# Final sums of a tile taken bank by bank, and two more places for gathered rows

## The chip, the cores and the metric

One core of one Trainium2 chip. The metric is the device time of one execution in microseconds, as the median of three runs. All numbers of the profile come from one profiled execution of the same program.

## What is computed

One step of an encoder layer for a prompt of 1024 tokens and a sample of 32. After a mixer (an RG-LRU and an mLSTM group, not touched here) comes a mixture of experts with product keys (PEER), then a final RMSNorm:

```python
x = x + g1 * (concat([ya, yb]) @ w_out)
h2 = rmsnorm(x, norm2_w) * (1 + sc2) + sh2
# peer(h2): for each token and each of 8 heads, 16 experts out of 16384
ue = take(u, expert, axis=0)                     # rows of 1024 floats
act = gelu(einsum('phkd,pd->phk', ue, xb))
ve = take(v, expert, axis=0)
out = einsum('phk,phkd->pd', g * act, ve)
y = rmsnorm(x + g2 * out, final_norm_w)
```

Here `g` is the softmax over the 16 chosen scores of a head. Each token reads 8 x 16 = 128 rows of `u` and 128 of `v`; the kernel keeps `u` and `v` of an expert side by side in one table, `peer_uv`, so that one gathered row has 2048 floats, 8 KB.

## The kernel before, in words

The tokens are nine tiles: eight of 128 prompt tokens and one of 32 sample tokens (`NT` = 9). The mixer runs first, for all tiles. After it comes one loop over **slots**, 128 for a prompt tile and 32 for the sample, 1056 in all, written out by each engine for itself in the same order. A slot is one gather by an indirect DMA into one **place** of SBUF: 128 rows, 32 tokens (a quad, `q` = 0 to 3) by four experts of one head, 1 MB. What a slot needs, in order:

- POOL (line 681) waits until the place is free and issues the gather. It waits on `v_free`, which PE counts up per slot, and, at a head's first slot, on `idx_ready`, the expert numbers.
- DVE (`dot`, line 1971) waits for the gather (`e_ld`) and forms the dot products of the 128 `u` rows with the tokens' rows, which stand in `xrep`, spread over the partitions.
- ACT (`weight`, lines 1371 to 1379) makes gelu times gate of it and writes the weights into a small diagonal (`diag`), then ups `dg_ready`.
- PE (`mix`, line 1030) multiplies the `v` halves of the rows by the diagonal with four matmuls and adds them up in PSUM. Quads 0 and 1 add up in bank 0, quads 2 and 3 in bank 1 (`q // 2`). Its last matmul ups `v_free`.

Each queue is in order: a wait of an engine holds everything behind it on that engine. Between the slots each engine has other work of the next tiles, placed by slot number: on DVE the steps that choose the experts (routing, lines 1883 to 1963, one head in 16 slots), on PE the query matmuls (`query`, line 966; scores, index turns) and the replicas (`replicate`, line 1017), which spread the rows of 32 tokens over 128 partitions by two matmuls of 512 columns; ACT copies each into `xrep` (line 1396) before PE makes the next.

The order of slots in a tile is set by `SETS`: for most tiles heads 0 to 3 with quads 0, 1, 2, 3, then heads 4 to 7 with quads 0, 1, 2, 3, each quad of a set being 16 slots. So bank 0 takes slots 0 to 31 and 64 to 95 of a tile, bank 1 slots 32 to 63 and 96 to 127. Tile 1 begins with sets of two heads, there bank 1 is first written in slot 16. `spans[t, i]` lists the slots of tile `t` that go to bank `i`.

There are `RING` = 6 places from the start and two more from slot `JOIN` = 118 on, when the weights that lay in `r_w` are used up; each slot takes the place that was used longest ago.

When a tile's slots are done, its sums go through `final_sum` (after the dot of slot 3 of the next tile; lines 1984 and 1990 are its multiply out of PSUM by `g2` and its add of the `x1` rows), `final_square` (after slot 4, line 1996, with the sum of squares per row), a sum over partitions by PE (`sum_squares`, line 1040, after slot 6), `final_variance` (slot 11), a root by ACT (slot 12), `final_scale` (slot 14, line 2010) and then, on SP (`finish`), eight stores of the tile in 1 KB pieces (line 577) and the loads of the next tile's `x1` rows into `x1s` (line 571). For tile 0 those loads stand on SP's queue behind four loads of query weights for tile 1, 1 MB each, and twelve small ones. The results are written over the tile's normed rows (`h2h(t, 0)` in `r_yT`, `h2h(t, 1)` in `r_vo`), which the replicas read.

What couples the tiles is in `final_sum` and `mix`:

```python
dve.wait_ge(v_free, RING + (t * TILE_SLOTS + TILE_SLOTS if nq == 4 else N_SLOTS))   # final_sum
last.then_inc(acc_free, 1)                       # behind the multiplies of both banks
if t and s == t * TILE_SLOTS:                    # mix, the tile's first slot
    pe.wait_ge(acc_free, t)
```

The line numbers are those of the kernel before; in the changed one they are a few higher (the dot is line 1976, the multiply 1990, the add 1994, the squares 2000, mix 1035, the gather 686).

## Time and profile before

| | us |
|---|---|
| median of three runs (3294.46 to 3301.82) | 3297.12 |
| the profiled execution's own time | 3296.16 |
| its span in the profile | 3294.3 |

The page of the profile gives, for each engine, the busy time as a share of the span; slices, 40 equal parts of the span with the busy share in tenths and the DMA rate; and groups of instructions by source line. Waits are listed by who waited for whom, with total, count and the longest one. A timeline lists single instructions with their start, length and, in brackets, how long the engine had been idle before and what ended that. A window gives the busy time of each engine in a stretch, TensorE's granted clock, the DMA engines' share and their rate. In all of them the places appear under the name of the SBUF tensor they lie in (`r_vo`, `r_yT`, `r_qk`, `r_w`).

### The profile page before, as it was taken

How to read it: one execution, taken by the hardware profiler on the slowest of the kernel's cores; microseconds unless marked ns; L12 is line 12 of the kernel's file. 1: busy time of each engine (PE TensorE's matmuls, PEld its weight loads, DVE VectorE, ACT ScalarE, POOL GpSimd, SP SyncE). 2: the span in 40 equal slices, each digit the busy share in tenths (PEclk: the TensorE clock that was granted, in tenths of full speed). 3: DMA queues.
4: the chain of work that ended last, by engine and by line, in shares of the span. 5: the costliest groups of instructions: out<-in, count | busy, mean ns of one | idle time of the engine just before them, and what ended most of it. 6: DMA issues, size and time to landing. Idle time of an engine off the chain costs nothing.

```text
span 3294.3 us, 46115 instructions
## 1 busy us (share of the span) xinstructions
PE 2306.9 (70%) x15134; PEld 1144.3 (35%) x15134; DVE 2219.6 (67%) x5518; ACT 2000.6 (61%) x6402; POOL 1215.7 (37%) x1118
## 2 busy tenths in 40 slices
PE   7999987988668666666666666666666666666544
PEld 5665464333234333333333233223333332232110
DVE  5687256877667767666766676667666766676645
ACT  3332055777666666666666666666666666666655
POOL 0000102344434444444444444444434444443433
PEclk9999997899656556555655565556556655565555
DMA  7232327999999999999999999999999999999998
GB/s 285 87 104 76 81 72 289 390 392 395 405 385 420 420 420 405 420 420 420 395 420 421 419 399 420 420 420 394 420 420 420 395 420 420 420 397 419 421 421 344
DMA packets 184164, 1195.13 MB, mean 363 GB/s; under 512 B 22122, under 2 KB 32906, under 8 KB 44530
## 3 DMA queue, kind: packets, MB, share of 16 engines
q0 software_dynamic: 154240, 1113.16, 82.5%
q1 hardware_dynamic: 29684, 79.02, 6.8%
q8 instruction: 120, 1.97, 0.3%
q14 instruction: 120, 0.98, 0.1%
HBM read 1182.83 MB, written 9.25 MB: 362 GB/s over the span
## 4 chain that ended last, share of the span: by engine, by line
DMA 49%; PE 24%; ACT 10%; DVE 8%; issue 5%; POOL 3%; SPq 1%; DVEq 0%; POOLq 0%; ACTq 0%
DMA r_w<-in_peer_uv,gidx 21%; DMA r_qk<-in_peer_uv,gidx 12%; DMA r_yT<-in_peer_uv,gidx 11%; PE ps L777 6%; PE ps L1030 5%; PE ps L834 3%; PE ps L966 3%; DMA r_vo<-in_peer_uv,gidx 3%; PE ps L926 2%; PE ps L1017 2%; DVE r_w L1971 2%; ACT mixc L1375 2%; POOL r_vo L681 2%; ACT mixc L1374 1%; DVE r_qk L1971 1%
## 5 line engine op out<-in xcount | busy, mean ns | idle before, releaser
L1371 ACT ACTIVATE mixc<-mixc 128x1 f32<-128x1 f32 x1056 | 212.4, 201 | 797.6 <-DVE r_qk L1971 212.0
L681 POOL DMA_INDIRECT r_vo<-in_peer_uv,gidx x273 | 337.9, 1238 | 647.4 <-PE ps L1030 591.1
L1030 PE MATMUL ps<-r_qk 128*32 128x256 f32 x2192 | 273.1, 587 | 374.9 <-ACT r_qk L1379 334.2
L681 POOL DMA_INDIRECT r_qk<-in_peer_uv,gidx x274 | 284.3, 1038 | 413.7 <-PE ps L1030 371.8
L1375 ACT ACTIVATE mixc<-mixc 128x1 f32<-128x1 f32 x1056 | 409.2, 388 | 35.2
L1030 PE MATMUL ps<-r_w,r_qk 128*32 128x256 f32 x1880 | 245.2, 614 | 250.1 <-ACT r_qk L1379 236.8
L681 POOL DMA_INDIRECT r_yT<-in_peer_uv,gidx x274 | 314.6, 1148 | 255.1 <-PE ps L1030 200.6
L1374 ACT ACTIVATE mixc<-mixc 128x1 f32<-128x1 f32 x1056 | 395.1, 374 | 1.0
L1379 ACT ACTIVATE r_qk<-prm,mixc 128x32 f32<-128x32 f32 x1056 | 340.3, 322 | 34.3
L681 POOL DMA_INDIRECT r_w<-in_peer_uv,gidx x235 | 245.4, 1044 | 276.3 <-PE ps L1030 258.2
L1030 PE MATMUL ps<-r_yT,r_qk 128*32 128x256 f32 x2192 | 230.7, 530 | 131.0 <-ACT r_qk L1379 116.4
L1372 ACT ACTIVATE mixc<-gate,mixc 128x1 f32<-128x1 f32 x1056 | 296.1, 280 | 0.0
L1030 PE MATMUL ps<-r_vo,r_qk 128*32 128x256 f32 x2184 | 214.7, 515 | 91.7 <-DVE r_vo L1984 46.7
L1971 DVE SCALAR_TENSOR_TENSOR r_vo<-r_vo,r_wq 128x1024 f32<-128x1024 f32 x137 | 167.8, 1225 | 130.9 <-DMA r_vo<-in_peer_uv,gidx 130.6
L1971 DVE SCALAR_TENSOR_TENSOR r_qk<-r_qk,r_wq 128x1024 f32<-128x1024 f32 x137 | 167.8, 1225 | 125.1 <-DMA r_qk<-in_peer_uv,gidx 120.9
L1030 PEld LDWEIGHTS ps<-r_qk 128*32 128x32 f32 x2192 | 54.8, 135 | 567.9 <-ACT r_qk L1379 472.7
L1971 DVE SCALAR_TENSOR_TENSOR r_vo<-r_vo,r_qk 128x1024 f32<-128x1024 f32 x136 | 166.5, 1224 | 117.0 <-DMA r_vo<-in_peer_uv,gidx 116.4
L1971 DVE SCALAR_TENSOR_TENSOR r_qk<-r_qk 128x1024 f32<-128x1024 f32 x137 | 167.8, 1225 | 102.7 <-DMA r_qk<-in_peer_uv,gidx 96.5
L777 PE MATMUL ps<-r_hT,r_w 128*128 128x384 f32 (+1 forms) x768 | 231.0, 462 | 1.8 <-DVE r_hT L1607 1.8
L1971 DVE SCALAR_TENSOR_TENSOR r_yT<-r_yT,r_wq 128x1024 f32<-128x1024 f32 x136 | 166.5, 1225 | 83.4 <-DMA r_yT<-in_peer_uv,gidx 79.8
L1971 DVE SCALAR_TENSOR_TENSOR r_w<-r_w,r_wq 128x1024 f32<-128x1024 f32 x118 | 144.6, 1226 | 111.9 <-DMA r_w<-in_peer_uv,gidx 104.4
L1971 DVE SCALAR_TENSOR_TENSOR r_yT<-r_yT,r_qk 128x1024 f32<-128x1024 f32 x138 | 168.8, 1224 | 73.7 <-DMA r_yT<-in_peer_uv,gidx 68.8
(331 smaller groups left out, 4297.1 us busy)
## 6 DMA issues: line engine op xcount, KB each, us to landing
r_w<-in_ada_w SPq DMA_DIRECT2D x18, 1024.0 KB, 5.4
r_w<-in_w_lin SPq DMA_DIRECT2D x16, 512.0 KB, 8.1
r_w<-in_peer_wq SPq DMA_DIRECT2D x6, 1024.0 KB, 24.2
r_hT<-in_peer_wq SPq DMA_DIRECT2D x6, 1024.0 KB, 21.8
r_yT<-in_peer_uv,gidx POOLq DMA_INDIRECT x274
r_qk<-in_peer_uv,gidx POOLq DMA_INDIRECT x274
r_vo<-in_peer_uv,gidx POOLq DMA_INDIRECT x273
r_vo<-in_x_prompt SPq DMA_DIRECT2D x8, 512.0 KB, 7.0
```

Of the source, the lines that this page charges most:

```text
L681: pool.indirect_dma_start(ring[i], None, table, bass.IndirectOffsetOnAxis(gidx_t[:, t % 2, h, c:c + 1], 0)).then_inc(e_ld[i], 16)
L777: m = nc.tensor.matmul(ps[:, bank, 0:n], wblk[:, nblk % 8, k, :], hT[:, k, c0:c0 + n], start=k == 0, stop=k == KD - 1)
L834: m = nc.tensor.matmul(ps[0:r, bank, :], hT[:, k, t * P:t * P + r], w[:, k, :], start=k == 0, stop=k == KD - 1)
L926: m = nc.tensor.matmul(ps[0:r, bank, :], y_tile(t, k), wout[:, c, k, :], start=k == 0, stop=k == KD - 1)
L966: mm = nc.tensor.matmul(ps[:, bank, c * P:(c + 1) * P], wq_tile(t, h, k, c), h2T[p][:, k, :], start=k == 0, stop=k == KD - 1)
L1030: mm = nc.tensor.matmul(ps[c * DEC:(c + 1) * DEC, q // 2, (q % 2) * QC:(q % 2 + 1) * QC], diag[:, s % 4, :], row[:, D + c * QC:D + (c + 1) ...
L1371: wch.mark(nc.scalar.activation(sq[:, i:i + 1], d, ACT.Square, scale=GELU_C ** 0.5 / TANH_K))
L1372: nc.scalar.activation(gd[:, i:i + 1], gate_t[t % 2][:, h, c:c + 1], ACT.Copy, scale=d)
L1374: wch.link(nc.scalar.activation(th[:, i:i + 1], sq[:, i:i + 1], ACT.Tanh, scale=d, bias=d))
L1375: wch.link(nc.scalar.activation(wc[:, i:i + 1], th[:, i:i + 1], ACT.Identity, scale=gd[:, i:i + 1], bias=gd[:, i:i + 1]))
L1379: nc.scalar.activation(diag[:, s % 4, :], sel32, ACT.Copy, scale=wc[:, i:i + 1]).then_inc(dg_ready, 1)
L1971: V.scalar_tensor_tensor(ring[i][:, 0:D], ring[i][:, 0:D], TANH_K, xrep[b % 2], ALU.mult, ALU.mult, accum_out=dots[:, i:i + 1]).then_inc(d ...
```

## The change

The sum of a tile is taken per bank. `final_half(t, 0)` stands after slot 101 of tile `t` itself and `final_squares(t, 0)` after slot 103; the halves of bank 1 stand after slots 3 and 5 of the next tile, with `final_variance` and all behind it as before. For tile 0 the half of bank 0 and its squares stand after slot 1 of tile 1. `acc_free` becomes two semaphores, and PE waits for a bank's own at that bank's first slot of a tile. Since a half writes over rows that replicas read, it waits for all replicas of the tile (`x_rep`). The chain of a tile has six steps in place of five, and PE's sum of squares moves from slot 6 to slot 8.

From slot 544 (slot 32 of tile 4) on there are ten places: 8 and 9 lie in `r_yT[:, 0:2048]` and in the first 2048 columns of `og` in `r_vo`, the rows of tiles 0 to 3. Their first use waits until all stores of these tiles have landed (`y_st`).

```diff
-PLACES = 8
-JOIN = 118
+PLACES = 10
+JOINS = {118: (6, 7), 4 * TILE_SLOTS + 32: (8, 9)}
-K_ROUTE, K_W, K_FIN = 14, 3, 5
+K_ROUTE, K_W, K_FIN = 14, 3, 6
-        mixc = sb("mixc", [P, 32])
+        mixc = sb("mixc", [P, 40])
         ring = [r_vo[:, 0:2048], r_yT[:, 4352:6400], r_yT[:, 6400:8448], r_qk[:, 4096:6144],
-                r_qk[:, 6144:8192], r_vo[:, 2048:4096], r_w[:, 4096:6144], r_w[:, 6144:8192]]
+                r_qk[:, 6144:8192], r_vo[:, 2048:4096], r_w[:, 4096:6144], r_w[:, 6144:8192],
+                r_yT[:, 0:2048], r_vo[:, NT * 516:NT * 516 + 2048]]
...
-            free += [(n - PLACES, RING + i) for i in range(PLACES - RING) if n == JOIN]
+            free += [(None, i) for i in JOINS.get(n, ())]
...
+        replicated = [sum(x[0] <= t for x in builds) for t in range(NT)]
...
                 elif i < RING:
                     pool.wait_ge(i_mm, (5, 0, 0, 7, 9, 9)[i])
+                elif i < 8:
+                    pool.wait_ge(o_mm, 2 * NT)
                 else:
-                    pool.wait_ge(o_mm, 2 * NT)
+                    pool.wait_ge(y_st, 128 * 4)
...
-                if t and s == t * TILE_SLOTS:
-                    pe.wait_ge(acc_free, t)
+                if t and s == spans[t, q // 2][0]:
+                    pe.wait_ge(acc_free[q // 2], t)
...
-                if t and j == 6:
+                if t and j == 8:
                     sum_squares(t - 1, 4)
...
-            def final_sum(t, nq):
-                fc.base, fc.n = t * K_FIN, 0
+            def final_half(t, i, nq):
+                if i == 0:
+                    fc.base, fc.n = t * K_FIN, 0
                 n = min(nq, 2)
-                parts = [h2h(t, i)[:, 0:n * QC].rearrange("p (q n) -> p q n", q=n) for i in range((nq + 1) // 2)]
-                dve.wait_ge(v_free, RING + (t * TILE_SLOTS + TILE_SLOTS if nq == 4 else N_SLOTS))
+                a = h2h(t, i)[:, 0:n * QC].rearrange("p (q n) -> p q n", q=n)
+                dve.wait_ge(v_free, RING + spans[t, i][-1] + 1)
+                dve.wait_ge(x_rep, 2 * replicated[t])
                 dve.wait_ge(g2_ld, 192)
-                for i, a in enumerate(parts):
-                    last = V.tensor_tensor(a, ps[:, i, 0:n * QC].rearrange("p (q n) -> p q n", q=n),
-                                           (g2b if nq == 4 else g2s).unsqueeze(1).broadcast_to([P, n, QC]), ALU.mult)
-                last.then_inc(acc_free, 1)
-                dve.wait_ge(acc_free, t + 1)
+                V.tensor_tensor(a, ps[:, i, 0:n * QC].rearrange("p (q n) -> p q n", q=n),
+                                (g2b if nq == 4 else g2s).unsqueeze(1).broadcast_to([P, n, QC]), ALU.mult).then_inc(acc_free[i], 1)
+                dve.wait_ge(acc_free[i], t + 1)
                 dve.wait_ge(x1_ld, t * 64 + 64)
-                for i, a in enumerate(parts):
-                    last = V.tensor_tensor(a, a, x1s[:, 2 * i:2 * i + n], ALU.add)
-                fc.mark(last)
+                fc.mark(V.tensor_tensor(a, a, x1s[:, 2 * i:2 * i + n], ALU.add))
...
+                if 0 < t < NT - 1 and j == 101:
+                    final_half(t, 0, 4)
+                if 0 < t < NT - 1 and j == 103:
+                    final_squares(t, 0, 4)
+                if t == 1 and j == 1:
+                    final_half(0, 0, 4)
+                    final_squares(0, 0, 4)
                 if t and j == 3:
-                    final_sum(t - 1, 4)
-                if t and j == 4:
-                    final_square(t - 1, 4)
+                    final_half(t - 1, 1, 4)
+                if t and j == 5:
+                    final_squares(t - 1, 1, 4)
```

How the instructions then stand. First DVE at the start of tile 1, from the dot of slot 1 on (the dots are the rows of 128x1024; lines 1896 to 1917 before and 1901 to 1922 with the change are routing steps). Before:

```order
L1971 SCALAR_TENSOR_TENSOR r_vo,mixc<-r_vo,r_qk 128x1024
L1902 MAX_INDEX r_qk<-r_qk 128x8 x2
L1903 TENSOR_TENSOR r_qk<-r_qk 128x256
L1971 SCALAR_TENSOR_TENSOR r_yT,mixc<-r_yT,r_qk 128x1024
L1909 MAX r_qk<-r_qk 128x8
L1911 RECIPROCAL r_qk<-r_qk 128x1
L1912 CAST r_qk<-r_qk 128x32
L1971 SCALAR_TENSOR_TENSOR r_yT,mixc<-r_yT,r_qk 128x1024
L1984 TENSOR_TENSOR r_yT<-ps,r_wr 128x512
L1984 TENSOR_TENSOR r_vo<-ps,r_wr 128x512
L1990 TENSOR_TENSOR r_yT<-r_yT,r_qk 128x512
L1990 TENSOR_TENSOR r_vo<-r_vo,r_qk 128x512
```

With the change:

```order
L1976 SCALAR_TENSOR_TENSOR r_vo,mixc<-r_vo,r_qk 128x1024
L1990 TENSOR_TENSOR r_yT<-ps,r_wr 128x512
L1994 TENSOR_TENSOR r_yT<-r_yT,r_qk 128x512
L2000 SCALAR_TENSOR_TENSOR r_qk<-r_yT 128x256 x2
L1907 MAX_INDEX r_qk<-r_qk 128x8 x2
L1908 TENSOR_TENSOR r_qk<-r_qk 128x256
L1976 SCALAR_TENSOR_TENSOR r_yT,mixc<-r_yT,r_qk 128x1024
L1914 MAX r_qk<-r_qk 128x8
L1916 RECIPROCAL r_qk<-r_qk 128x1
L1917 CAST r_qk<-r_qk 128x32
L1976 SCALAR_TENSOR_TENSOR r_yT,mixc<-r_yT,r_qk 128x1024
L1990 TENSOR_TENSOR r_vo<-ps,r_wr 128x512
```

One multiply, one add and two of the four squares stand behind the second dot instead of the fourth, ahead of the dots of slots 2 and 3.

Then DVE at the start of tile 4, from the dot of slot 3 on. Before:

```order
L1971 SCALAR_TENSOR_TENSOR r_yT,mixc<-r_yT,r_qk 128x1024
L1984 TENSOR_TENSOR r_yT<-ps,r_wr 128x512
L1984 TENSOR_TENSOR r_vo<-ps,r_wr 128x512
L1990 TENSOR_TENSOR r_yT<-r_yT,r_qk 128x512
L1990 TENSOR_TENSOR r_vo<-r_vo,r_qk 128x512
L1902 MAX_INDEX r_qk<-r_qk 128x8 x2
L1903 TENSOR_TENSOR r_qk<-r_qk 128x256
L1971 SCALAR_TENSOR_TENSOR r_qk,mixc<-r_qk 128x1024
L1996 SCALAR_TENSOR_TENSOR r_qk<-r_yT 128x256 x2
```

With the change:

```order
L1976 SCALAR_TENSOR_TENSOR r_yT,mixc<-r_yT,r_qk 128x1024
L1990 TENSOR_TENSOR r_vo<-ps,r_wr 128x512
L1994 TENSOR_TENSOR r_vo<-r_vo,r_qk 128x512
L1907 MAX_INDEX r_qk<-r_qk 128x8 x2
L1908 TENSOR_TENSOR r_qk<-r_qk 128x256
L1976 SCALAR_TENSOR_TENSOR r_qk,mixc<-r_qk 128x1024
L1914 MAX r_qk<-r_qk 128x8
L1916 RECIPROCAL r_qk<-r_qk 128x1
L1917 CAST r_qk<-r_qk 128x32
L1976 SCALAR_TENSOR_TENSOR r_w,mixc<-r_w,r_qk 128x1024
L2000 SCALAR_TENSOR_TENSOR r_qk<-r_vo 128x256 x2
```

Bank 1's half of the sum stays behind slot 3; its squares move from behind slot 4 to behind slot 5; bank 0's half is gone from here.

Last DVE with the change from the dot of slot 101 of tile 4 on, where there were only the dots and the routing steps before:

```order
L1976 SCALAR_TENSOR_TENSOR r_yT,mixc<-r_yT,r_qk 128x1024
L1990 TENSOR_TENSOR r_yT<-ps,r_wr 128x512
L1994 TENSOR_TENSOR r_yT<-r_yT,r_qk 128x512
L1921 MAX_INDEX r_qk<-r_qk 128x8
L1922 MATCH_REPLACE r_qk<-r_qk 128x256
L1976 SCALAR_TENSOR_TENSOR r_vo,mixc<-r_vo,r_qk 128x1024
L1926 TENSOR_SCALAR r_qk<-r_qk 128x1
L1927 MAX r_qk<-r_qk 128x8
L1976 SCALAR_TENSOR_TENSOR r_vo,mixc<-r_vo,r_qk 128x1024
L2000 SCALAR_TENSOR_TENSOR r_qk<-r_yT 128x256 x2
```

The multiply and the add of bank 0 stand behind the dot of slot 101, its two squares behind that of slot 103.

## Rows read from the trace of the kernel before

**Rows 1.** The page: busy time, and GB/s of the DMA engines in 40 slices.
```profile
PE 2306.9 (70%) x15134; PEld 1144.3 (35%) x15134; DVE 2219.6 (67%) x5518; ACT 2000.6 (61%) x6402; POOL 1215.7 (37%) x1118
...
GB/s 285 87 104 76 81 72 289 390 392 395 405 385 420 420 420 405 420 420 420 395 420 421 419 399 420 420 420 394 420 420 420 395 420 420 420 397 419 421 421 344
```

**Rows 2.** Windows: length, PE, PEld, DVE, ACT, POOL busy, clock, DMA share, GB/s.
```profile
2000.00:2200.00 200.00, 129.76 (x936) 61.63 (x940) 136.91 (x352) 132.78 (x447) 85.39 (x79) 0.59 1.01 420
1250.00:1262.00 12.00, 8.11 (x70) 2.88 (x74) 11.57 (x36) 6.34 (x23) 8.34 (x6) 0.64 0.93 369
1576.00:1592.00 16.00, 11.62 (x82) 4.90 (x83) 14.98 (x46) 8.88 (x33) 10.34 (x8) 0.50 0.86 338
1904.00:1918.00 14.00, 10.45 (x76) 3.74 (x77) 12.98 (x42) 8.24 (x29) 9.46 (x7) 0.50 0.89 346
2228.00:2242.00 14.00, 7.74 (x50) 2.37 (x50) 12.34 (x39) 7.25 (x26) 6.49 (x4) 0.50 0.80 315
2558.00:2572.00 14.00, 9.28 (x70) 3.17 (x74) 13.81 (x43) 7.80 (x30) 8.61 (x6) 0.50 0.83 322
2886.00:2898.00 12.00, 8.37 (x58) 2.77 (x62) 11.86 (x38) 6.52 (x24) 7.55 (x5) 0.50 0.83 326
3212.00:3226.00 14.00, 9.47 (x74) 3.07 (x74) 11.27 (x24) 8.38 (x30) 7.93 (x6) 0.59 0.91 359
936.00:946.00 10.00, 8.41 (x87) 5.68 (x87) 9.83 (x24) 8.61 (x33) 5.28 (x4) 0.84 0.86 324
```

**Rows 3.** Waits of the core: total us, times, longest us.
```profile
PE ps L1030 <- DVE r_vo L1984: 46.7, 8, 9.0
...
DVE r_yT L1990 <- DMA r_qk<-x_dram: 7.9, 1, 7.9
```

**Rows 4.** Timeline, start of tile 5: start, us, instruction, [idle before <- releaser].
```profile
2224.08 1.08 PE L1030 MATMUL ps<-r_qk 128*32 128x256 f32 x8 [3.23 <-ACT r_qk L1379]
...
2230.09 1.23 DVE L1971 SCALAR_TENSOR_TENSOR r_yT<-r_yT,r_qk 128x1024 f32<-128x1024 f32 x1 [1.52 <-DMA r_yT<-in_peer_uv,gidx]
...
2231.25 0.69 DVE L1984 TENSOR_TENSOR r_yT<-ps,r_wr 128x512 f32<-128x512 f32 x1
...
2232.68 1.93 PE L1030 MATMUL ps<-r_vo,r_qk 128*32 128x256 f32 x16 [5.44 <-DVE r_vo L1984]
...
2234.55 2.11 POOL L681 DMA_INDIRECT r_vo<-in_peer_uv,gidx  x1 [8.06 <-PE ps L1030]
```

**Rows 5.** Groups of DVE, the squares: busy us, mean ns, idle before.
```profile
L1996 DVE SCALAR_TENSOR_TENSOR r_qk<-r_yT 128x256 bf16<-128x256 f32 x16 | 6.8, 424 | 0.3
```

**Rows 6.** Timeline about slot 101 of tile 4.
```profile
2149.99 2.07 PE L1017 MATMUL ps<-r_vo,spread 32*128 32x512 f32 x2 [1.47 <-ACT r_wq L1396]
...
2154.20 1.23 DVE L1971 SCALAR_TENSOR_TENSOR r_w<-r_w,r_qk 128x1024 f32<-128x1024 f32 x1 [0.77 <-DMA r_w<-in_peer_uv,gidx]
```

**Rows 7.** Timeline about the start of tile 1.
```profile
912.88 0.41 DVE L1903 TENSOR_TENSOR r_qk<-r_qk 128x256 f32<-128x256 f32 x1
...
927.86 0.69 DVE L1990 TENSOR_TENSOR r_yT<-r_yT,r_qk 128x512 f32<-128x512 f32 x1 [7.92 <-DMA r_qk<-x_dram]
...
932.67 1.08 PE L1030 MATMUL ps<-r_qk 128*32 128x256 f32 x8 [6.78 <-ACT r_qk L1379]
...
933.67 5.26 PE L966 MATMUL ps<-r_wq,r_hT 128*128 128x128 f32 x32
...
939.80 0.94 POOL L681 DMA_INDIRECT r_w<-in_peer_uv,gidx  x1 [4.31 <-PE ps L1030]
```

**Rows 8.** DMA queues in 910 to 914: packets, MB, share of 16 engines.
```profile
q0 software_dynamic: 183, 1.34, 90.9%
q1 hardware_dynamic: 181, 0.15, 12.7%
```

**Rows 9.** Timeline of SP, first store of tile 3; SP's queue in 1936 to 1950.
```profile
1933.24 0.32 SPq L577 DMA_DIRECT2D out<-r_yT  x1
...
q1 hardware_dynamic: 682, 0.57, 12.0%
```

More of the change, by code:

```diff
@@ L284, in build @@
         e_ld = [sem(f"e_ld{j}") for j in range(PLACES)]
-        dot_done, dg_ready, v_free, acc_free = (sem(n) for n in ("dot_done", "dg_ready", "v_free", "acc_free"))
+        dot_done, dg_ready, v_free = (sem(n) for n in ("dot_done", "dg_ready", "v_free"))
+        acc_free = [sem(f"acc_free{i}") for i in range(2)]
         s_tr, s_ev = sem("s_tr"), sem("s_ev")
@@ L1975, in y_quads, with final_squares @@
                 return [h2h(t, q // 2)[:, q % 2 * QC:(q % 2 + 1) * QC] for q in range(nq)]
-            def final_sum(t, nq):
-                fc.base, fc.n = t * K_FIN, 0
+            def final_half(t, i, nq):
+                if i == 0:
+                    fc.base, fc.n = t * K_FIN, 0
                 n = min(nq, 2)
-                parts = [h2h(t, i)[:, 0:n * QC].rearrange("p (q n) -> p q n", q=n) for i in range((nq + 1) // 2)]
-                dve.wait_ge(v_free, RING + (t * TILE_SLOTS + TILE_SLOTS if nq == 4 else N_SLOTS))
+                a = h2h(t, i)[:, 0:n * QC].rearrange("p (q n) -> p q n", q=n)
+                dve.wait_ge(v_free, RING + spans[t, i][-1] + 1)
+                dve.wait_ge(x_rep, 2 * replicated[t])
                 dve.wait_ge(g2_ld, 192)
-                for i, a in enumerate(parts):
-                    last = V.tensor_tensor(a, ps[:, i, 0:n * QC].rearrange("p (q n) -> p q n", q=n),
-                                           (g2b if nq == 4 else g2s).unsqueeze(1).broadcast_to([P, n, QC]), ALU.mult)
-                last.then_inc(acc_free, 1)
-                dve.wait_ge(acc_free, t + 1)
+                V.tensor_tensor(a, ps[:, i, 0:n * QC].rearrange("p (q n) -> p q n", q=n),
+                                (g2b if nq == 4 else g2s).unsqueeze(1).broadcast_to([P, n, QC]), ALU.mult).then_inc(acc_free[i], 1)
+                dve.wait_ge(acc_free[i], t + 1)
                 dve.wait_ge(x1_ld, t * 64 + 64)
-                for i, a in enumerate(parts):
-                    last = V.tensor_tensor(a, a, x1s[:, 2 * i:2 * i + n], ALU.add)
-                fc.mark(last)
-            def final_square(t, nq):
+                fc.mark(V.tensor_tensor(a, a, x1s[:, 2 * i:2 * i + n], ALU.add))
+            def final_squares(t, i, nq):
                 fc.need()
-                for q, a in enumerate(y_quads(t, nq)):
+                for q in range(2 * i, min(2 * i + 2, nq)):
+                    a = y_quads(t, nq)[q]
                     last = V.scalar_tensor_tensor(fdump, a, 1.0, a, ALU.mult, ALU.mult, accum_out=fss[:, q:q + 1])
@@ L1998, in final_square @@
                         fc.link(last)
-                last.then_inc(f_sq, 1)
+                    else:
+                        last.then_inc(f_sq, 1)
             def final_variance(t, nq):
@@ L2007, in final_scale @@
                 fc.link(V.reciprocal(frs[:, 0:nq], frs[:, 0:nq]))
-                assert fc.n == nq + 1
+                assert fc.n == (K_FIN if nq == 4 else 2)
                 for q, a in enumerate(y_quads(t, nq)):
@@ L2134, in _ @@
                         copy_places(m)
-            final_sum(NT - 1, 1)
-            final_square(NT - 1, 1)
+            final_half(NT - 1, 0, 1)
+            final_squares(NT - 1, 0, 1)
             final_variance(NT - 1, 1)
```

## Prediction

> **What bounds the kernel now.** I read the page's slices first. From the 13th slice on the DMA engines bring about 420 GB/s, except in one slice of about four, which shows 394 to 405, and the last; PE, DVE, ACT and POOL are busy for 70%, 67%, 61% and 37% of the span, so none is the limit of the loop [rows 1]. A stretch of 200 us inside it shows the 16 DMA engines at a share of 1.01 and 420 GB/s [rows 2]. A slot gathers 128 rows of 8 KB, 1.049 MB, so it costs 1.049/0.420 = 2.50 us whatever the other engines do. What can be won is time in which the DMA engines have too little to do.
>
> Where that is, the waits say. PE waited eight times for the multiply of the final sum, 46.7 us in all; DVE waited once, 7.9 us, for rows of `x1_dram` [rows 3]. Eight is the number of tile ends. The start of tile 5 shows the mechanism [rows 4]. DVE does the dot of slot 3 at 2230.09, then the two multiplies that empty the banks (0.69 us each). Only then, at 2232.68, does PE mix slot 0, although its mix before that had started at 2224.08. POOL, which needs the place that PE frees, goes on at 2234.55 after 8.06 us of idling, and by then the queue of gathers has run dry: 2228 to 2242 shows 315 GB/s [rows 2].
>
> I price each such hole as its window times the missing share of 420 GB/s [rows 2]: 12 x 51/420 = 1.5 us at tile 2, 16 x 82/420 = 3.1 at tile 3, 14 x 74/420 = 2.5 at tile 4, 14 x 105/420 = 3.5 at tile 5, 14 x 98/420 = 3.3 at tile 6, 12 x 94/420 = 2.7 at tile 7, 14 x 61/420 = 2.0 at the sample tile. The sum is 18.6 us. The other thing that lowers the rate once a tile is the store and load of 1 KB pieces, which the change leaves alone.
>
> **The bank split, tiles 2 to 8.** Bank 0 gets its last slot of a tile as slot 95. Its half of the sum moves to slots 101 and 103, so that `acc_free[0]` is up long before PE comes to the next tile's slot 0. Bank 1 is written first in slot 32 of the next tile (16 in tile 1) and is emptied after slot 3. PE waits for neither: in tile 5 it would mix slot 0 right behind the mix of 2224.08, and POOL would go on at its pace of one gather in 2.5 us. Gain: all of the 18.6 us, if nothing takes the wait's place. The work on DVE is the same, four operations of 0.69 us and four squares of 0.42 us a tile [rows 4, 5]; the chain has one step more. Half of it, 1.4 + 1.0 = 2.4 us with the reads of the accumulator, now stands at slots 101 to 103. DVE is busy for 137 us of 200 [rows 2], 1.7 us of each 2.5, so its spare 0.8 us a slot takes this in over three slots, while the gathers in flight cover a pause: at tile 5 POOL idled 8.1 us and only 3.5 were lost, so some 4.6 cost nothing. Cost: nothing; without that cover it would be 2.4 us for each of seven tiles, 17 us.
>
> DVE's new waits at slot 101: bank 0's mixes ended with slot 95, the `x1` rows were asked for at slot 14, and the last replica of the tile's rows ended at 2149.99 + 2.07 = 2152.06, while the dot of slot 101 began at 2154.20 [rows 6]. All are met by then. The last would have to be late by those 2.1 us and a dot of 1.2 before DVE stopped at all.
>
> **The start of tile 1.** Here the change adds a wait. Tile 0's bank 0 is summed after slot 1 instead of slot 3, and its add needs the `x1` rows, which came only at 927.86, after 7.92 us of idling [rows 7]. They stand on SP's queue behind 4 MB of query weights. In 910 to 914 that queue had 181 packets against 183 of the gathers [rows 8]: it is served in turn, so that more gathers in flight do not make the rows later. I keep 927.9. Behind DVE's stop now stand the dots of slots 2 and 3 too. Before, PE's mix of slot 4 began 4.8 us after the rows had come, at 932.67; the query matmuls (5.26 us) held slot 5's, and POOL issued the gather behind that at 939.80 [rows 7]. With the change the same chain has more in it ahead of slot 4: two squares with their reads, 1.0 us; the dots of slots 2 and 3, 2 x 1.2; the multiply of bank 1's half, 0.7; and two routing steps more, 1.5 together by my estimate (the largest operation in them takes 0.41 [rows 7]). Sum 5.6 us, by which the gather of 939.80 comes later. Slots 0 and 1 are mixed some 6 us earlier and their two gathers go out early, but no more of them than before are out ahead of this point, and the engines ran short here already: 936 to 946 shows 324 GB/s, 2.3 us lost [rows 2]. Bounds: the early gathers fill most of it (2 us), or the delay and the 2.3 us again are lost (8). I take 5.5, nearest to the delay itself.
>
> **Two more places.** From slot 544 on, ten gathers can be out or in use instead of eight. With eight the DMA share in the steady stretch is 1.01 [rows 2], so I cost them at nothing: they make the queue longer, not the engines faster. They are a second cover for the last four holes (3.5 + 3.3 + 2.7 + 2.0 = 11.5 us), which the split has closed already. Their own wait: POOL issues into place 9 for slot 544 once tile 3 is stored. Slot 14 of tile 4 released the stores, the first at 1933.24 [rows 9], and POOL is at slot 544 ten slots later, at about 1958. A tile's store is 0.52 MB, the first on that queue, and it moved 0.57 MB from 1936 to 1950 [rows 9]: the stores are down some 8 us ahead. Cost zero; if they were late, the other eight places would cover about 4.6 us.
>
> The Trainium skill (DMA: Bandwidth & Descriptors, Where 436 GB/s comes from) gives 435.2 GB/s as the ceiling of the SBUF ports. By that figure a slot could take 1.049/0.4352 = 2.41 us, an estimate, and if depth were what is missing, 512 slots with two more places would save 512 x 0.09 = 46 us. The long window at 420 GB/s shows no such rate with eight places; with ten no row shows it.
>
> **Sum.** The profiled execution took 3296.16 us: 3296.16 - 18.6 + 5.5 = 3283.1. The median of the runs, 3297.12, lies 1.0 above it, so **3284 us**, 0.4% less. A measurement of this kernel tells about 0.2% (6.6 us) from no change.
>
> **Rivals.**
> - *The start of tile 1 costs nothing.* The two gathers that go out early bridge the later stop. For: the loads of SP fill the engines during the first part of DVE's stop. Against: the query matmuls stand in PE's order right behind slot 4. Time: 3297.1 - 18.6 = 3278.5. Chance 0.16.
> - *Half of the holes stay.* DVE still does 1.4 us after slot 3 and squares after slot 5, beside routing steps, and slots 0 to 6 come in a bunch. For: in 1250 to 1262 DVE is busy for 11.6 of 12 us [rows 2]. Against: a good part of that is the work that moves to slot 101, and 4.6 us of pause are covered. Time: 3297.1 - 9.3 + 5.5 = 3293.3, mostly within 0.2%. Chance 0.21.
> - *Slower: DVE stops at slot 101.* The place is its wait for the replicas: PE makes the last one only after ACT has copied the half before it, and that copy stands behind ACT's weight of slot 98. Every dot is queued behind DVE's wait, and PE and POOL behind the dots. A stop costs time only beyond the 4.6 us that the gathers in flight cover; from there on it decides. To turn a gain of 13.1 us into a loss of 8, seven stops must lose 3 us each, so last some 7.6 us. Time 3305. For: it is the one new wait whose margin is a few us. Against: that margin, [rows 6]. Chance 0.06.
> - *Depth raises the rate.* The best slice of the page has 421 GB/s, the steady window 420; but slices mix in what is below it. Were the last 512 slots to run at 425, they would save 512 x 2.50 x 5/425 = 15 us more: 3269. Against: a share of 1.01. Chance 0.04.
>   The Trainium skill's ceiling (the section named above) would make of this case 46 us less instead of 15, again an estimate.
> - My forecast, 3284: chance 0.53.
>
> **How the numbers follow.** The forecast's own bounds are 3297.1 - 18.6 + 2 = 3280.5 and, with 8, 3286.5, and a median scatters by 2 to 3 us. The range takes in the first two rivals: 3277 to 3293.5. Left out are the slower case, the faster rate and the far side of the second rival. Faster by over 0.2% is below 3290.5: the forecast, the first and the fourth rival and a little of the second (0.53 + 0.16 + 0.04 + 0.03 = 0.76); the rest of the second, 0.18, lies within; slower has 0.06.
>
> **What would show it.** PE's wait for the DVE multiply is gone or stands once; the windows at the seven tile starts read 410 GB/s or more; the one wait for `x_dram` grows from 7.9 us to 13 to 15 and stands between slots 1 and 2, and the place behind it loses 5 to 10 us instead of 2.3; the steady rate is 420 before and behind slot 544, and POOL doesn't stop there. Wrong would be: 350 GB/s or less left at tiles 2 to 4, a wait of DVE ahead of the half sum in slot 101, or a steady rate above 424 in the last four tiles.

## The result, and the profile after

The change makes the kernel **slower**: 3304.05 us (3297.42 to 3308.96) against 3296.98 us (3292.29 to 3303.93) for the kernel before, 20 runs each, ratio 1.0020 with a 95% interval of 1.0014 to 1.0027. That is 7 us more, where I had forecast 3284 and a range up to 3293.5. The profiled execution took 3305.01 us, span 3303.3.

In the profile after, what I wanted to see is there. The waits, total, times, longest:

```profile
DVE r_yT L1994 <- DMA r_qk<-x_dram: 11.3, 1, 11.3
...
PE ps L1035 <- DVE r_yT L1990: 6.2, 1, 6.2
DVE r_yT L1990 <- DMA r_wr<-in_final_norm_w: 3.6, 1, 3.6
```

PE waits for a multiply of the final sum once, 6.2 us, where it waited eight times, 46.7 us [rows 3]. And here are the windows in which I had counted my gain (columns as in [rows 2]), with the start of tile 1 last:

```profile
1250.00:1262.00 12.00, 9.37 (x56) 2.98 (x60) 10.44 (x32) 7.83 (x30) 5.21 (x5) 0.50 1.02 420
1576.00:1592.00 16.00, 11.13 (x68) 3.18 (x68) 14.12 (x46) 10.42 (x39) 7.27 (x6) 0.50 1.01 424
1904.00:1918.00 14.00, 10.05 (x60) 2.98 (x60) 11.54 (x38) 9.44 (x34) 6.34 (x5) 0.50 1.01 423
2228.00:2242.00 14.00, 9.61 (x60) 2.73 (x52) 10.22 (x31) 9.89 (x30) 3.86 (x4) 0.50 1.01 417
2558.00:2572.00 14.00, 9.26 (x56) 2.92 (x60) 11.47 (x35) 9.03 (x32) 5.28 (x6) 0.50 1.01 420
2886.00:2898.00 12.00, 8.96 (x52) 2.75 (x52) 10.15 (x32) 7.39 (x29) 3.65 (x4) 0.50 1.02 423
3212.00:3226.00 14.00, 9.18 (x44) 2.19 (x44) 7.47 (x13) 8.18 (x29) 4.84 (x5) 0.50 1.01 421
930.00:946.00 16.00, 12.04 (x84) 7.27 (x84) 15.79 (x41) 11.17 (x41) 4.69 (x4) 0.63 0.48 180
```

All seven holes (a hole is a stretch at a tile's start in which the mean rate dips) are filled: 417 to 424 GB/s where there were 315 to 369. Only the last window, at the start of tile 1, is worse: a share of 0.48, so the engines idled for 0.52 x 16 = 8.3 us. So by my way of counting the kernel should have gained 18.6 us and lost some 7.

The plainest clock in this kernel is the start of each slot's dot, since the loop can't go faster than its gathers land. Read from both timelines, for the same slot (slots counted through from 0, so that 128 is the first of tile 1):

| dot of slot | before, us | after, us | later by |
|---|---|---|---|
| 129 | 911.19 | 910.85 | -0.3 |
| 130 | 914.39 | 930.20 | 15.8 |
| 132 | 929.86 | 935.08 | 5.2 |
| 141 | 945.98 | 953.25 | 7.3 |
| 256 | 1240.30 | 1248.07 | 7.8 |
| 512 | 1895.16 | 1902.64 | 7.5 |
| 640 | 2222.05 | 2230.07 | 8.0 |
| 1024 | 3204.66 | 3213.55 | 8.9 |
| 1055, the last | 3284.19 | 3293.15 | 9.0 |

The whole loss is made between slots 129 and 141. After that some 900 slots go at one pace in both, through seven holes in one kernel and none in the other: the changed kernel even loses 1.7 us more. The start of tile 1, timeline after:

```profile
915.65 0.69 DVE L1990 TENSOR_TENSOR r_yT<-ps,r_wr 128x512 f32<-128x512 f32 x1 [3.57 <-DMA r_wr<-in_final_norm_w]
...
927.68 0.69 DVE L1994 TENSOR_TENSOR r_yT<-r_yT,r_qk 128x512 f32<-128x512 f32 x1 [11.33 <-DMA r_qk<-x_dram]
...
930.20 1.22 DVE L1976 SCALAR_TENSOR_TENSOR r_yT<-r_yT,r_qk 128x1024 f32<-128x1024 f32 x1
...
935.08 1.21 DVE L1976 SCALAR_TENSOR_TENSOR r_qk<-r_qk 128x1024 f32<-128x1024 f32 x1
```

DVE stops between the dots of slots 129 and 130, first for the constants, then for the `x1` rows, 14.9 us in all; the rows come at 927.7 as before. What that does to the gathers shows on POOL, after and then before (slots 136 to 139):

```profile
918.37 0.94 POOL L686 DMA_INDIRECT r_vo<-in_peer_uv,gidx  x1 [8.62 <-PE ps L1035]
919.61 0.94 POOL L686 DMA_INDIRECT r_vo<-in_peer_uv,gidx  x1 [0.30 <-issue]
936.82 1.88 POOL L686 DMA_INDIRECT r_yT<-in_peer_uv,gidx  x1 [16.27 <-PE ps L1035]
939.01 0.94 POOL L686 DMA_INDIRECT r_yT<-in_peer_uv,gidx  x1 [0.30 <-PE ps L1035]
```
```profile
921.96 0.94 POOL L681 DMA_INDIRECT r_vo<-in_peer_uv,gidx  x1 [11.62 <-PE ps L1030]
923.20 0.94 POOL L681 DMA_INDIRECT r_vo<-in_peer_uv,gidx  x1 [0.30 <-issue]
925.33 0.94 POOL L681 DMA_INDIRECT r_yT<-in_peer_uv,gidx  x1 [1.19 <-PE ps L1030]
926.58 0.94 POOL L681 DMA_INDIRECT r_yT<-in_peer_uv,gidx  x1 [0.30 <-issue]
```

Before, four gathers go out before the rows have come. After, two do; the next two come some 12 us later, because the mixes that free their places need the dots of slots 130 and 131, and these now stand behind the stop. So the engines run empty.

Where the filled holes went shows at the end. Windows after, then before:

```profile
3280.00:3285.00 5.00, 2.17 (x16) 0.40 (x16) 2.46 (x4) 2.80 (x11) 0.00 (x0) 0.50 0.47 197
3285.00:3290.00 5.00, 2.17 (x16) 0.40 (x16) 2.47 (x4) 2.78 (x11) 0.00 (x0) 0.50 0.12 48
3290.00:3295.00 5.00, 2.17 (x16) 0.40 (x16) 2.47 (x4) 2.80 (x11) 0.00 (x0) 0.50 0.03 13
```
```profile
3275.00:3280.00 5.00, 2.17 (x24) 0.40 (x16) 2.49 (x5) 2.75 (x10) 0.00 (x0) 0.50 1.01 419
3280.00:3285.00 5.00, 2.19 (x24) 0.40 (x16) 2.54 (x5) 2.75 (x10) 0.00 (x0) 0.50 0.28 115
```

After, the engines taken as a mean have all but finished at 3285, and the dots go on for 8 us more, each still waiting for its gather and 2.5 us behind the last:

```profile
3288.20 1.23 DVE L1976 SCALAR_TENSOR_TENSOR r_yT<-r_yT,r_wq 128x1024 f32<-128x1024 f32 x1 [1.27 <-DMA r_yT<-in_peer_uv,gidx]
...
3290.70 1.23 DVE L1976 SCALAR_TENSOR_TENSOR r_vo<-r_vo,r_wq 128x1024 f32<-128x1024 f32 x1 [1.26 <-DMA r_vo<-in_peer_uv,gidx]
...
3293.15 1.23 DVE L1976 SCALAR_TENSOR_TENSOR r_vo<-r_vo,r_wq 128x1024 f32<-128x1024 f32 x1 [1.22 <-DMA r_vo<-in_peer_uv,gidx]
```

A share of 0.12 and then 0.03 of sixteen engines is about two engines at work and then less than one. If a gather's 128 rows of 8 KB fall evenly on the sixteen engines, each has 8 of them, and 8 x 0.311 = 2.49 us, the pace of the dots (single packets show 0.309 to 0.32 us in the trace). The gather has landed when the last engine has its part. If one engine is behind, the dots go by it, and the other fifteen run ahead. I counted how far, from the packets of the traces: the gathered rows moved when a dot starts, divided by 128, less the gathers landed. Before, this lead is 1.1 gathers at slot 255, 1.97 at slot 643, in the middle of tile 5's hole, and 0.55 at slot 650, behind it. The hole took 1.42 x 2.49 = 3.5 us of it, just the 3.5 us that I had priced it at. After, no hole takes the lead away: 1.75 at slot 255, 2.9 at 639, 3.6 at 800, 4.0 at 1050. So in a hole the fast engines wait for the slow one, and without holes they do that waiting at the end.

The dots say the same. From ten slots ahead of a tile's start to its slot 30, tiles 2 to 8 taken together, they take 733.4 us before and 734.5 us after.

**Theory A**: the most loaded DMA engine sets the pace; holes in the mean rate cost nothing as long as that engine has work, and the 7 us are the stop in tile 1. **Theory B**, my prediction's: the mean rate decides, the holes were worth 18.6 us, and something else in the change (the two places, or the steps moved) ate that.

### The profile page after: what moved, and what is told of

It reads as the page before. It is cut to its first block, busy times and chain, and to the rows that moved or that the text cites. A ratio compares the mean times of both kernels' runs of the same rounds, so it can differ in the third digit from the quotient of the medians.

```text
span 3303.3 us, 46146 instructions
## 1 busy us (share of the span) xinstructions
PE 2305.8 (70%) x15134; PEld 1136.3 (34%) x15134; DVE 2219.8 (67%) x5518; ACT 1997.1 (60%) x6402; POOL 1200.0 (36%) x1118
## 3 DMA queue, kind: packets, MB, share of 16 engines
q8 instruction: 120, 1.97, 0.3%
## 4 chain that ended last, share of the span: by engine, by line
DMA 52%; PE 26%; ACT 9%; DVE 8%; issue 3%; POOL 1%; SPq 1%; DVEq 0%; POOLq 0%; ACTq 0%
DMA r_qk<-in_peer_uv,gidx 14%; DMA r_w<-in_peer_uv,gidx 13%; DMA r_vo<-in_peer_uv,gidx 13%; DMA r_yT<-in_peer_uv,gidx 9%; PE ps L782 6%; PE ps L1035 5%; PE ps L971 4%; PE ps L839 3%; PE ps L1022 2%; PE ps L931 2%; ACT mixc L1380 2%; DVE r_qk L1976 1%; ACT mixc L1379 1%; DVE r_vo L1976 1%; DMA r_qk<-x_dram 1%
## 5 line engine op out<-in xcount | busy, mean ns | idle before, releaser
L686 POOL DMA_INDIRECT r_yT<-in_peer_uv,gidx x299 | 340.7, 1139 | 366.2 <-PE ps L1035 316.8
L1035 PE MATMUL ps<-r_qk 128*32 128x256 f32 x1984 | 238.8, 570 | 271.1 <-ACT r_qk L1384 271.0
L1035 PE MATMUL ps<-r_yT,r_qk 128*32 128x256 f32 x2392 | 270.8, 551 | 197.7 <-ACT r_qk L1384 197.5
L686 POOL DMA_INDIRECT r_qk<-in_peer_uv,gidx x248 | 265.9, 1072 | 369.3 <-PE ps L1035 335.5
L1035 PE MATMUL ps<-r_vo,r_qk 128*32 128x256 f32 x2400 | 261.4, 545 | 156.2 <-ACT r_qk L1384 149.9
L1035 PE MATMUL ps<-r_w,r_qk 128*32 128x256 f32 x1672 | 206.7, 594 | 207.5 <-ACT r_qk L1384 207.5
L686 POOL DMA_INDIRECT r_w<-in_peer_uv,gidx x209 | 223.6, 1070 | 278.3 <-PE ps L1035 256.6
L1976 DVE SCALAR_TENSOR_TENSOR r_vo<-r_vo,r_qk 128x1024 f32<-128x1024 f32 x150 | 183.5, 1223 | 118.2 <-DMA r_vo<-in_peer_uv,gidx 118.0
L1022 PE MATMUL ps<-r_vo,spread 32*128 32x512 f32 x168 | 155.9, 1024 | 99.5 <-ACT r_wq L1401 59.3
L1976 DVE SCALAR_TENSOR_TENSOR r_qk<-r_qk 128x1024 f32<-128x1024 f32 x124 | 151.7, 1223 | 92.7 <-DMA r_qk<-in_peer_uv,gidx 87.4
## 6 DMA issues: line engine op xcount, KB each, us to landing
r_qk<-in_ada_w SPq DMA_DIRECT2D x2, 2048.0 KB, 16.6
```

The lines of the kernel that those rows point to most:

```text
L686: pool.indirect_dma_start(ring[i], None, table, bass.IndirectOffsetOnAxis(gidx_t[:, t % 2, h, c:c + 1], 0)).then_inc(e_ld[i], 16)
L1022: nc.tensor.matmul(ps[:, 2, :], spread[q, :], h2h(t, c)[q, :], start=True, stop=True).then_inc(x_rep, 1)
L1035: mm = nc.tensor.matmul(ps[c * DEC:(c + 1) * DEC, q // 2, (q % 2) * QC:(q % 2 + 1) * QC], diag[:, s % 4, :], row[:, D + c * QC:D + (c + 1) ...
L1976: V.scalar_tensor_tensor(ring[i][:, 0:D], ring[i][:, 0:D], TANH_K, xrep[b % 2], ALU.mult, ALU.mult, accum_out=dots[:, i:i + 1]).then_inc(d ...
```

## The experiments

Medians are of 5 to 12 runs of each kernel; the ratio is to the kernel before, run beside it. Where dots of two profiles are compared, mind that each kernel has one profile and that the loop does not begin at the same instant in all: the dot of slot 112, where none of the edits has acted yet, lies between 4.2 us earlier and 6.1 us later than before. So what counts is the length between two dots.

### One part of the change alone

The change without its two places (`PLACES = 8`, `JOINS = {118: (6, 7)}`).

> The change without its two more places: eight places to the end, the sums still taken per bank. The changed kernel took 3304 us, the one before 3297. Theory A (a gathered row block has landed only when the slowest of the sixteen DMA engines has done its part, so the holes in the mean rate at the starts of tiles 2 to 8 cost nothing, and the 7 us come from the later work of VectorE at the start of tile 1, where dot 130 starts 15.8 us later than before): 3304 us, within 2 of it. Theory B (the holes did cost time, some 18 us in all as I predicted, and something in the change, above all the two more places from slot 544 on, ate that again): 3304 less what the places cost, 3286 to 3297 us.

Measured 3302.08 us, ratio 1.0014 (1.0005 to 1.0023). The interval overlaps the change's own; by the medians the places cost 2 us, not the 7 to 18 of B's forecast. The stretches about the seven tile starts take 733.5 us in its profile, as in the kernel before (733.4), though its holes are filled and it has no more places. Its lead at slot 1050 is 2.2 gathers, not 4.0, and from slot 141 to the last dot it takes 4.3 us less than the change with its places.

The kernel before with the two places alone:

```diff
-PLACES = 8
-JOIN = 118
+PLACES = 10
+JOINS = {118: (6, 7), 4 * TILE_SLOTS + 32: (8, 9)}
...
+                else:
+                    pool.wait_ge(y_st, 128 * 4)
```

> The kernel before with the two more places alone, from slot 544 on; the sums stay whole, so PE still waits for VectorE's multiply at each tile's start. Theory A: 3297 us, within 2, though the holes of tiles 5 to 8 in the mean rate (354 to 382 GB/s in their 20 us windows) get shorter or vanish, and in the last 15 us the mean rate falls off earlier while dots still come at about 2.49 us each. Theory B: the holes of tiles 5 to 8 are worth 3.5, 3.3, 2.7 and 2.0 us, so up to 11.5 us less: 3285.5 us.

Measured 3298.83 us, ratio 1.0003 (0.9994 to 1.0012): nothing. Its windows at the starts of tiles 5 to 8, then those of tiles 5 and 6 in the kernel before:

```profile
2220.00:2240.00 20.00, 10.01 (x64) 3.25 (x60) 16.15 (x52) 12.40 (x41) 6.20 (x6) 0.53 1.01 419
2560.00:2580.00 20.00, 15.97 (x137) 9.37 (x127) 18.06 (x51) 12.29 (x45) 11.60 (x9) 0.67 0.97 388
2886.00:2898.00 12.00, 7.97 (x66) 2.76 (x66) 11.86 (x37) 6.53 (x23) 6.82 (x5) 0.64 0.90 327
3212.00:3226.00 14.00, 8.86 (x74) 2.96 (x74) 11.27 (x24) 8.36 (x30) 7.71 (x6) 0.62 0.83 327
```
```profile
2220.00:2240.00 20.00, 10.67 (x68) 3.25 (x60) 16.16 (x52) 12.45 (x40) 7.82 (x6) 0.50 0.87 351
2560.00:2580.00 20.00, 16.37 (x138) 8.88 (x138) 17.82 (x51) 11.84 (x44) 12.63 (x9) 0.62 0.89 354
```

The hole of tile 5 is gone here and that of tile 6 smaller (351 and 354 GB/s before); those of tiles 7 and 8 stay, at 327 GB/s each where [rows 2] have 326 and 359. No dot behind the two filled holes has gained: the loop began 1.3 us earlier than before (slot 129), and slots 560 and 768 are 0.7 and 0.6 us earlier, slot 1024 0.2 us later. The lead was 3.9 gathers at slot 1024, 2.9 at slot 1050. B had forecast 11.5 us; for what really changed its pricing gives 20 x 68/420 + 20 x 34/420 = 4.9 us, less 14 x 32/420 = 1.1 at tile 8, so 3.8, and the interval allows a gain of 2.

One thing that the medians can't tell shows in the dots. From slot 512 to slot 1024 all five kernels with ten places take longer than the kernel before (1309.5 us): by 1.4 (the change), 1.3, 1.5, 2.2 and 1.7 us; the three with eight places and nothing that costs time there differ by -0.8 (the split alone), +0.3 and -0.3. So two more places seem to cost one to two microseconds. Why is open.

### The start of tile 1 put back

```diff
-                if t == 1 and j == 1:
+                if t == 1 and j == 3:
                     final_half(0, 0, 4)
+                if t == 1 and j == 5:
                     final_squares(0, 0, 4)
```

> The change with one thing put back: the sum of tile 0's first bank comes after slot 3 of tile 1 and its squares after slot 5, as in the other tiles, not after slot 1. Theory A: nearly all of the loss goes, since dot 141 and all behind it were 7.3 us late or more by that step alone: 3296 to 3298 us, level with the kernel before and no faster, though the holes of tiles 2 to 8 stay filled. Theory B (as in the prediction, the filled holes are worth 18.6 us): 3278 to 3279 us.

Measured 3296.27 us, ratio 1.000 (0.999 to 1.001). One half sum moved back by two slots, its squares with it, takes away the whole loss of the change, to within the 3 us of the interval. The seven holes are still filled, tile 5's for one:

```profile
2228.00:2242.00 14.00, 7.95 (x50) 1.84 (x50) 12.03 (x33) 7.86 (x28) 6.42 (x6) 0.50 1.01 420
```

and they are worth nothing. The two forecasts lay 17 us apart, so B falls here.

### The rows that DVE waits for, loaded first

On SP, ahead of tile 1, in the kernel before and in the change:

```diff
-            for h in range(4):
-                load_wq(1, h)
...
+            load_x1(0, 4, x1_dram[0:P])
             for c in range(4):
...
+            for h in range(4):
+                load_wq(1, h)
```

> The kernel before, with one order on SP changed: at the start of tile 1 it loads tile 0's x1 rows and the constants for the sum ahead of the four query-weight loads, not behind them. Both theories: VectorE's wait of 7.92 us for the x1 rows at slot 3 of tile 1 goes or nearly goes. Theory A: the dots behind it come that much earlier, less what the weights' later arrival costs, since at that point the whole ring stands full and no DMA engine works: 3289 to 3294 us. Theory B (only the holes at the starts of later tiles count, and this stop is taken up by work that runs behind it): 3297 us.

> The change, with SP loading tile 0's x1 rows and the constants of the sum ahead of the four query-weight loads of tile 1. In the kernel before this order alone took 3 us off (3293.5). Theory A: VectorE's wait of 11.3 us for the x1 rows goes, and with it all of the change's loss, since there is no other: 3292 to 3295 us, level with the kernel before in the same order. Theory B, holes worth 18.6 us and hidden so far behind something at tile 1: 3275 us. A third reading, that the places or the sums per bank cost a few microseconds of their own: 3297 to 3300 us.

In the kernel before: 3293.47 us, ratio 0.9985 (0.9977 to 0.9994), the fastest of all. In the change: 3295.45 us, ratio 0.9989 (0.9980 to 0.9998), 0.5 us above A's range and 20 from B's. Its loss is gone, and no gain of the holes appears. In both, DVE's wait for `x_dram` stands in no row any more. Window of the kernel before with this order:

```profile
936.00:946.00 10.00, 6.81 (x34) 3.07 (x34) 5.85 (x14) 7.88 (x22) 3.96 (x4) 0.50 1.02 423
```

The window that showed 324 GB/s [rows 2] is full. Though the stop of 7.9 us is gone and the dot of slot 132 comes 11.4 us earlier than before, slot 141's is only 2.0 and slot 256's 2.2 earlier. By the packets, 2.2 of the 4 MB of weights now come after 910 us and none did before, and dots wait for gathers again. What is won, 3.1 us by the medians, is near the 2.3 us in which engines idled in that window, and not the 7.9 of the stop: the order of transfers gave back idle time of the engines, as far as these numbers tell, and not the stop. (A's own reason, that no engine works during the stop, does not hold: in 914:920 and 920:926 of the kernel before the share is 1.02 and 1.03, and the idling comes behind them.)

Both edits together, in the change:

> Both mendings together: the change with tile 0's first bank summed after slot 3 of tile 1 and its squares after slot 5, and the x1 rows loaded ahead of the query weights. Theory A: 3292 to 3295 us, since either mending alone already takes the stop away and the rest costs and gives nothing. Theory B: 3275 us.

Measured 3295.25 us, ratio 0.9995 (0.9986 to 1.0004): level, 0.3 us above A's range, two mendings of one fault.

### Longer holes

In the kernel before, from tile 2 on, the sum one or two slots later, its squares and their matmul with it:

```diff
-                if t and j == 3:
+                if t and j == (3 if t == 1 else 4):
                     final_sum(t - 1, 4)
```

> The kernel before with its holes made longer: in tiles 2 to 8 the sum of the finished tile comes after slot 4, not slot 3 (squares after slot 5, their matmul at slot 7); tile 1 is left as it was. Each of the seven holes grows by one slot, 2.5 us. Theory A: at tile 5 the first gather after the hole is issued at 2234.55 us and the dot that needs it, the ninth of the tile, would come at about 2222.05 + 8 x 2.49 = 2242 us; a slot later leaves 5 us for a transfer that takes 2.5 us on its own, so nothing or nearly nothing is lost: 3297 to 3299 us. Theory B (a hole is lost rate): 7 x 2.5 = 17 us more at most, 3305 to 3314 us.

> The same with the sum after slot 5 (squares after slot 6, their matmul at slot 8): each hole grows by two slots, 5 us. Theory A: the first gather after the hole is issued about 2239.5 us at tile 5 for a dot due at 2242 us, so it is now late by some 2 us at each tile and DMA engines run dry: 3305 to 3313 us. So theory A has a step between slot 4 and slot 5. Theory B: 7 x 5 = 35 us more at most, twice the loss of slot 4: 3315 to 3332 us.

Measured: slot 4, 3303.46 us, ratio 1.0017 (1.0008 to 1.0026), 5.6 us, 0.8 a hole; slot 5, 3320.64 us, ratio 1.0063 (1.0049 to 1.0077), 21 us, 3.0 a hole. PE's waits for the multiply, slot 4 and slot 5:

```profile
PE ps L1030 <- DVE r_vo L1984: 64.4, 8, 10.2
```
```profile
PE ps L1030 <- DVE r_vo L1984: 81.7, 8, 12.3
```

46.7, 64.4 and 81.7 us of waiting are nearly equal steps (17.7 and 17.3). The cost of a hole goes 0 (from the change's filled holes to slot 3), 0.8, then 2.2 more, of 2.5 that the slot lasts. That is no straight line through all three, which B needs, but one that bends close behind the place where the kernel before stands, and beyond the bend a hole costs nearly its full length. A's numbers were too low at both (0 to 2 against 5.6 us, 8 to 16 against 21), B's held the second and not the first (8 to 17 forecast, 5.6 measured).

The place of the bend shows in the packets. A gather's first packets start some 2.5 us after POOL begins the issue (at tile 5 before: 2234.55 [rows 4], and the engines fill again from 2237 on), which A had left out. And I counted the engines that have a packet of a gather under way. In the holes of the kernel before their number falls to 7, 2, 2, 1, 1, 2 and 5 (tiles 2 to 8), never to none. With the sum at slot 4 it falls to one or two in every hole. At slot 5 there is none for 1.0 to 1.9 us in each of the seven. So the kernel before stands just ahead of the point where the last engine runs out of work too. The 0.8 us lost with slot 4 this count does not explain.

### One engine loaded, all engines loaded

This measures A's claim by itself. SP gets extra loads that nothing uses, into a buffer idle by then:

```diff
+                if 4 <= t < 8:
+                    sp.wait_ge(y_st, 128 * t)
+                    for m in range(16):
+                        sp.wait_ge(dot_done, t * TILE_SLOTS + 37 + 5 * m)
+                        sp.dma_start(r_yT[0:1, 0:2048], A["peer_uv"][m:m + 1]).then_inc(extra, 16)
+                        sp.wait_ge(extra, 16 * (16 * (t - 4) + m + 1))
```

The second kernel has one transfer of sixteen rows a tile instead of the loop, the third has 32 rows a tile, 2.5 slots apart.

> The kernel before with extra loads that nothing uses: in tiles 4 to 7 SP loads sixteen single rows of 8 KB a tile, one at a time, five slots apart, into a buffer that is idle by then: 64 packets of 8 KB in all, 512 KB. Theory A says that the dots go at the pace of the most loaded DMA engine. If a one-row transfer always falls to the same engine, that engine gets 64 x 0.31 = 20 us of work more, and the time rises by 10 to 20 us (less what that engine was ahead of the slowest one). If such transfers go round the engines, each gets 1.2 us, and the time rises by 1 to 2 us. Theory B, the mean rate decides, and holes in it are room: 512 KB at 420 GB/s, 1.2 us, whatever the engines: 3298 us.

> The same extra bytes, 512 KB, as four transfers of sixteen rows, one a tile, so that every DMA engine gets four packets of 8 KB. Theory A and theory B alike: 4 x 0.31 = 1.2 us more, 3298 us. If the kernel with one-row transfers is slower than this one by over 5 us, the load of a single engine sets the pace; if the two are level, either one-row transfers go round the engines or the mean rate decides.

> The single-row transfers doubled: thirty-two rows of 8 KB a tile in tiles 4 to 7, 128 in all, 1 MB. With sixteen a tile the profile showed one DMA engine each of whose steps grew by 0.31 us at every such row (about 5 us a tile), while the dots from slot 512 to slot 1024 came no later than before. Between those slots the dots of the kernel before take 1309.5 us where 512 gathers at 2.486 us take 1272.8, so the slowest engine has 36.7 us of other work there; about 17 us of it is the stores and x1 rows of four tiles, which every engine has. Theory A: the engine of the single rows could take up to about 20 us more before it became the slowest, which the 20 us of the first run just used up; with 40 us the time rises by about 20 us over that run, 3312 to 3322 us. Theory B, the mean rate: 1 MB at 420 GB/s, 2.5 us: 3299 to 3301 us.

| extra loads | bytes | us | ratio (95%) | dot 1024 less dot 512, against before |
|---|---|---|---|---|
| 64 of one row | 0.5 MB | 3299.40 | 1.0006 (0.9996 to 1.0016) | -0.3 us |
| 128 of one row | 1 MB | 3316.76 | 1.0058 (1.0044 to 1.0071) | +20.1 us |
| 4 of sixteen rows | 0.5 MB | 3303.36 | 1.0018 (1.0009 to 1.0027) | +4.5 us |

First, do single rows go to one engine? The trace doesn't name the engine of a packet. But each gather ends with sixteen small packets, and they fall into sixteen chains, one per engine, whose members follow each other by about 2.49 us; a longer step is other work. Followed through tile 4, one of the sixteen chains steps 0.3 us too far at 1999.5, 2012.2, 2025.0, 2037.7, 2048.0, 2063.2 and so on; the rows were moved at 1997.0, 2010.3, 2022.8, 2034.9, 2047.4, 2060.7. From one of these to the next lies each time a whole number of steps and 0.3 us, so it is the same chain. (The Trainium skill has both halves of this, in DMA: Bandwidth & Descriptors, Why a DMA increments its semaphore by 16 and not by 1. The engines of one transfer finish independently, and the semaphore counts them. A transfer issued from SP uses as many engines as its shape allows, always the lowest-numbered ones. The trace agrees: a row is one packet of 8 KB, and one chain has them all, at 0.31 us a row.)

The first 20 us on that engine cost nothing that the dots show, the second 20 cost 20.1 us. With 64 rows alone B looked right (3298 forecast, 3299.4 measured), and A's 10 to 20 us more did not come: it had named what that engine was ahead of the slowest one, but not put a number to it. With 128 rows 1 MB is 2.5 us by the mean rate, so B is out by a factor of eight, and A's forecast of 3312 to 3322, made with the slack that the first run had shown, holds the 3316.8. The loss comes where A wants it: the four tiles take 4.0, 5.8, 4.6 and 5.7 us more, and 3.9 to 4.2 us of each fall between its slots 64 and 112, while its rows are being moved. Windows of 240 us in tile 4, of the kernel before, with 64 rows and with 128 rows:

```profile
1960.00:2200.00 240.00, 158.63 (x1156) 78.01 (x1159) 163.72 (x423) 160.14 (x539) 102.26 (x95) 0.60 1.01 420
```
```profile
1960.00:2200.00 240.00, 158.78 (x1156) 78.34 (x1160) 162.90 (x420) 159.64 (x538) 101.77 (x95) 0.60 1.01 419
```
```profile
1960.00:2200.00 240.00, 158.83 (x1144) 80.78 (x1144) 160.97 (x413) 157.03 (x529) 99.38 (x93) 0.60 1.01 417
```

The mean hardly tells them apart (420, 419, 417 GB/s, share 1.01 in all), while the third has lost dots (x413 DVE operations against 423). That is why the rate of a window had shown me none of this.

## Why the prediction was wrong, point by point

- **The price of a hole**, "I price each such hole as its window times the missing share of 420 GB/s", 18.6 us in seven terms: this is the step that failed, all of it. The rate of the windows was right, and so was that the split fills them. But the rate is a mean over sixteen engines, and a gather is as late as its last engine. Measured worth of the seven: 0 (the change with tile 1 put back, 1.000, and 0.999 at best, 3 us; the dots about the seven tile starts, 733.4 us with holes and 733.5 without, both with eight places).
- The opening sentence, "What can be won is time in which the DMA engines have too little to do", needed "the slowest of". The trace of before had the sign, and I didn't look: straight across the hole of tile 5 the dots of slots 643 [rows 4] and 650 start at 2230.09 and 2247.47, 17.38/7 = 2.48 us apart as a mean, no slower than in a full stretch. A hole that costs 3.5 us would show there.

```profile
2247.47 1.23 DVE L1971 SCALAR_TENSOR_TENSOR r_yT<-r_yT,r_qk 128x1024 f32<-128x1024 f32 x1 [0.65 <-DMA r_yT<-in_peer_uv,gidx]
```

- "At tile 5 POOL idled 8.1 us and only 3.5 were lost, so some 4.6 cost nothing", which I used as cover at slot 101, had the right idea and stopped half way: the gathers in flight hid all of the 8.1.
- **The start of tile 1**, +5.5 us with bounds 2 and 8: the mechanism held in its main links. DVE stopped between slots 1 and 2 for 14.9 us (the forecast 13 to 15 was for the wait for `x_dram` alone, which is 11.3), the rows came at 927.68 (927.9), the place behind lost 8.3 us (5 to 10), and the gather issued at 939.80 before is issued at 944.97 (5.2 us later, forecast 5.6). What it left out are the gathers of slots 138 and 139, which used to go out ahead of the rows and now wait 11.5 and 12.4 us longer; "no more of them than before are out ahead of this point" should have said two fewer. The size was 7 to 8 us: dot 141 was 7.3 us late, the median 7. The upper bound, "the delay and the 2.3 us again are lost", was the nearer one. I had not foreseen that 3.6 of the 14.9 us are for the constants, which stand behind the same weights.
- **DVE at slot 101**: no wait stands there in the profile after, as forecast. **Two more places**: nothing that the medians tell, as forecast (1.0003 alone), one to two microseconds by the dots; POOL didn't stop at slot 544. But they are not the "second cover for the last four holes" that the prediction has: alone they filled one, half filled the next and left two.
- **The rivals.** None of the four names what happened. "Slower" named 3305 us, near the 3304 measured, but by a stop at slot 101 that did not occur. The rival that was missing is: the holes are worth nothing because an engine is behind, 3297.1 + 5.5 = 3302.6. Its evidence was in the rows.
- The Trainium skill's 435.2 GB/s (DMA: Bandwidth & Descriptors, Where 436 GB/s comes from): no stretch of 50 us in the loop of any trace came over 422.1 GB/s, with ten places neither.

Settled: that the stop in tile 1 is all of the loss within 3 us (moved by two slots, or its rows loaded earlier, it is gone), that filled holes give nothing the runs can tell, and that load on one engine counts in full once it is the slowest. Argued from traces only: which engine is slowest in the kernel before, and that the loads of instructions make it so. In tile 4 the chains' single longer steps are about 0.65 and 1.5 us, on one engine and then on another, and the page of the kernel before counts 120 packets of instructions of each size (16 KB and 8 KB); no kernel changed those.
